# Starting the value projection on the first half of the features while the second half of the modulation row is still being summed

## What is computed

```python
cond = silu(c)                                   # one row of 2048
mod = cond @ mod_w[i] + mod_b[i]                 # 2048 x 6144, per layer i
shift, scale, gate = split(mod, 3)
h = rms_norm(x, norm_g[i]) * (1.0 + scale) + shift
# layer 0, pool_branch(h, w_in, w_grp, layer_scale, w_out):
v, gate_p = split(h @ w_in, 2)                   # 2048 -> 2 x 2048
pooled = window_mean(v) - v                      # four groups, windows 2, 4, 8, 16
mixed = per_group(pooled @ w_grp) * layer_scale  # four 512 x 512 matrices
x = x + gate * ((mixed * silu(gate_p)) @ w_out)
```

## Time and profile before

| | us |
|---|---|
| time, median of 3 runs | 2393.55 (2393.16 to 2394.4) |
| the profiled execution's own time | 2394.16 |
| its span | 2392.2 |
| PE busy | 2336.1 (98% of the span) |
| DVE busy | 1525.3 (64%) |
| ACT busy | 1116.2 (47%) |
| mean granted TensorE clock | 0.989 of full |

### The profile page before, as it was taken

The page is one execution under the profiler, slowest core; times in us unless marked ns, Lnnn a source line. Parts: engine busy times, 40 slices in busy tenths (PEclk is TensorE's granted clock), DMA queues, the critical chain, the costliest instruction groups (busy, mean ns, idle before and its releaser), DMA issues.

```text
span 2392.2 us, 29822 instructions
## 1 busy us (share of the span) xinstructions
PE 2336.1 (98%) x10938; PEld 1897.4 (79%) x10938; DVE 1525.3 (64%) x1837; ACT 1116.2 (47%) x1346; POOL 15.2 (1%) x21
## 2 busy tenths in 40 slices
PE   5999999999999999999999999998999999999997
PEld 1877777888788878888888888887888888888886
DVE  2988897666697566865664444655655565565555
ACT  2454445444444555545545444454544444444444
POOL 0000000000000000000000000000000000000000
PEclk8999998999999999999999999999999999999999
DMA  9999996555697545756455766555556656656653
GB/s 393 389 374 383 373 400 228 179 185 175 199 391 250 153 172 182 233 162 185 150 176 148 235 196 190 188 190 170 186 189 189 193 185 193 191 183 193 191 186 105
DMA packets 245077, 528.18 MB, mean 221 GB/s; under 512 B 20956, under 2 KB 21220, under 8 KB 241000
## 3 DMA queue, kind: packets, MB, share of 16 engines
q1 hardware_dynamic: 241376, 510.40, 64.3%
q0 software_dynamic: 1936, 13.67, 1.5%
q10 hardware_dynamic: 1656, 2.65, 0.3%
HBM read 520.35 MB, written 6.30 MB: 220 GB/s over the span
## 4 chain that ended last, share of the span: by engine, by line
PE 94%; DVE 2%; DMA 2%; ACT 1%; issue 1%; SPq 0%; DVEq 0%; ACTq 0%
PE ps L1890 29%; PE ps L1892 29%; PE ps L1891 29%; PE ps L1959 3%; DMA T<-in_mod_w 1%; PE ps L1989 1%; PE ps L2158 0%; DMA raw<-in_pool_w_in 0%; DVE w_lo L1040 0%; PE ps L2199 0%; PE ps L2060 0%; PE ps L2135 0%; ACT tmp L797 0%; PE ps L2201 0%; PE ps L2200 0%
## 5 line engine op out<-in xcount | busy, mean ns | idle before, releaser
L1040 DVE TENSOR_TENSOR w_lo<-raw,w_hi 128x1024 fp32r<-128x1024 f32 x784 | 945.4, 1218 | 480.7 <-ACT w_hi L514 464.3
L514 ACT CAST w_hi<-raw 128x1024 fp32r<-128x1024 f32 x784 | 814.8, 1046 | 832.1 <-PE ps L1892 798.8
L1890 PE MATMUL ps<-w_hi,xa_hi 128*128 128x512 f32 x2176 | 858.2, 394 | 6.1 <-DVE xa_lo L1074 2.7
L1892 PE MATMUL ps<-w_hi,xa_lo 128*128 128x512 f32 x2176 | 849.5, 390 | 0.0
L1891 PE MATMUL ps<-w_lo,xa_hi 128*128 128x512 f32 x2176 | 848.8, 390 | 0.0
L1890 PEld LDWEIGHTS ps<-w_hi,xa_hi 128*128 128x128 f32 x2176 | 409.6, 188 | 100.0 <-issue 11.2
L1892 PEld LDWEIGHTS ps<-w_hi,xa_lo 128*128 128x128 f32 x2176 | 409.3, 188 | 86.1
L1891 PEld LDWEIGHTS ps<-w_lo,xa_hi 128*128 128x128 f32 x2176 | 409.8, 188 | 82.7
L1890 PE MATMUL ps<-w_hi,xb_hi 128*128 128x512 f32 x928 | 365.6, 394 | 1.5 <-issue 1.1
L1892 PE MATMUL ps<-w_hi,xb_lo 128*128 128x512 f32 x928 | 361.8, 390 | 0.0
L1891 PE MATMUL ps<-w_lo,xb_hi 128*128 128x512 f32 x928 | 361.6, 390 | 0.0
(11 more groups left out here) (257 smaller groups left out, 963.8 us busy)
## 6 DMA issues: line engine op xcount, KB each, us to landing
raw<-in_w_in SPq DMA_DIRECT2D x176, 512.0 KB, 4.3
T<-in_mod_w SPq DMA_DIRECT2D x160, 512.0 KB, 7.6
...
raw<-in_w_up SPq DMA_DIRECT2D x128, 512.0 KB, 4.3
raw<-in_w_down SPq DMA_DIRECT2D x128, 512.0 KB, 4.4
...
```

What stands on the lines that cost most here:

```text
L514: nc.scalar.copy(w_hi[:, o % SPL, :, 0:cols], raw[:, o % RAW, :, 0:cols]).then_inc(hi_ready, 1)
L1040: tt(w_lo[:, o % SPL, :, part], raw[:, o % RAW, :, part], w_hi[:, o % SPL, :, part].bitcast(F32), ALU.subtract).then_inc(lo_ready, 1)
L1890: mm(dst, x_hi, h, start=first and k == 0, stop=False)
L1892: ins = mm(dst, x_lo, h, start=False, stop=last and k == KPC - 1)
```

## The change

It does five things.

1. The scale row is summed in 32 pieces of 512 KB: 16 for its first half (features 0 to 1023), then 16 for its second half, each in PE matmuls of 256 columns, in a ring of 8 slots. The value phase begins when the first half is there. Its first 16 chunks are reordered: features 0 to 1023 of column blocks 0 and 1 (places 0 to 3 and 4 to 7), then features 1024 to 2047 of both. The 16 pieces of the second half stand on PE behind places 0, 1, 2, 3 and 5, and the copy, columns and scale of the second half behind places 5 to 8.
2. The rotary tables are computed on DVE at the chunks 3 to 5, and their sines on ACT at chunk 8, no longer ahead of the scale row.
3. The rides of DVE begin at chunk 8 (before: 4) and those of the first row end at chunk 36 (before: 31). Of PE's rides 6 stand in `group` (before: 8).
4. The shift comes later: its totals stand behind chunk 37 (before: 33), its columns behind chunk 38 (before: 34), and `shift0` runs at the end of `group` and in the first block of `pool_gate`.
5. `awake(n)` puts n matmuls of 128 columns, whose result is not used, on PE: in the start, around the first transposes of `norm1`, and ahead of and behind the first transposes of the last norm, `norm3`.

```diff
--- before
+++ after
@@ -68,10 +68,11 @@
 def _rides():
     first = {name: PHASES[name][0] * CPB for name in ("pool_v", "group", "pool_gate")}
     v, gate = first["pool_v"], first["pool_gate"]
-    at = [v + c for c in range(4, 32) for _ in range(2 if c in (11, 17, 23, 28) else 1)]
+    at = [v + c for c in range(8, 32) for _ in range(2 if c in (13, 19, 25) else 1)]
+    at += [first["group"] + c for c in range(5)]
     at += [gate + i * 9 // 8 for i in range(32)]
     at += [gate + 36 + i * 27 // 32 for i in range(32)]
-    return at, [first["group"] + i for i in range(8)] + [gate + 1 + i * 60 // 24 for i in range(24)]
+    return at, [first["group"] + i for i in range(6)] + [gate + i * 62 // 26 for i in range(26)]
 
 
...
@@ -368,10 +369,15 @@
 
             mws = [mod_w[i].rearrange("(p k) (u n) -> p u k n", k=KC, n=D) for i in range(2)]
             sp.dma_start(csil[:], c[0].rearrange("(p k) -> p k", k=KC)).then_inc(c_landed, 16)
-            for k in range(KC):
-                if k >= 4:
-                    sp.wait_ge(mod_taken, k - 3)
-                sp.dma_start(mod_raw[:, k % 4, :], mws[0][:, 1, k, :]).then_inc(mod_landed[k % 4], 16)
+            def scale_piece(p):
+
+                if p >= 8:
+                    sp.wait_ge(mod_taken, p - 7)
+                c0 = p // KC * (D // 2)
+                sp.dma_start(mod_raw[:, p % 8, :], mws[0][:, 1, p % KC, c0:c0 + D // 2]).then_inc(mod_landed[p % 8], 16)
+
+            for p in range(KC):
+                scale_piece(p)
...
@@ -405,9 +411,15 @@
                 for b in range(n):
                     for j in range(CPB):
                         g = (B0 + b) * CPB + j
-                        load(SOURCES[name], b, j, B0 + b, first=g < RAW)
+                        if g < 2 * CPB:
+                            load(lambda b, j: SOURCES["pool_v"](g // 4 % 2, g // CPB * 4 + g % 4), b, j, B0 + b, first=g < RAW)
+                        else:
+                            load(SOURCES[name], b, j, B0 + b)
+                        if 2 <= g < 7:
+                            for p in range(KC + (0, 4, 7, 10, 13)[g - 2], KC + (4, 7, 10, 13, 16)[g - 2]):
+                                scale_piece(p)
                         for q in range(len(RIDE_CHUNK)):
-                            if g == (RAW - 1, RAW - 1, RAW + 2, RAW + 4)[q] if q < 4 else g == RIDE_CHUNK[q - 4] + RAW:
+                            if g == (RAW - 1, RAW - 1, RAW, RAW + 4)[q] if q < 4 else g == RIDE_CHUNK[q - 4] + RAW:
                                 ride_first(q)
                         for q in range(len(PE_CHUNK)):
                             if g == PE_ISSUE[q]:
...
+            blk(0, {2: norm0_start, 8: rotary_sines, 9: lambda: norm0(2)})
+            blk(1, {3: lambda: norm0(3), 7: lambda: pool_v(0), 9: lambda: pool_job(0)})
+            pool_v(1)
+            for b in range(2, 4):
+                blk(b, {6: lambda: pool_job(b - 1)})
+                pool_v(b)
 
             B0, A0, _ = PHASES["group"]
 
             def mixed(g):
-                act.wait_ge(mod_taken, KC + (2 if g < 2 else 4))
+                act.wait_ge(mod_taken, 2 * KC + (2 if g < 2 else 4))
                 evac(T1[:, :, g * NBLK:g * NBLK + NBLK], A0 + g, B0 * CPB + 2 * g + 2)
 
             def shift0(g):
                 act.wait_ge(shifted, g + 1)
-                nc.scalar.copy(XA[0][:, 4 * g:4 * g + 4, :], (tmp[:], stage_f)[g % 2]).then_inc(xh_ready, 1)
+                nc.scalar.copy(FIRST[0][:, 4 * g:4 * g + 4, :], (tmp[:], stage_f)[g % 2]).then_inc(xh_ready, 1)
 
             for o in range(AHEAD, CPB + AHEAD):
                 hi(B0, o)
...
@@ -1258,16 +1276,16 @@
                 step(ts(MODB[i], MODB[i], 1.0, None, ALU.add))
             dve.wait_ge(csil_ready, 1)
 
-            def scale_rows(i, bank, taken, of=mod_taken):
+            def scale_rows(bank, taken, of, at=0, n=NBLK):
 
                 dve.wait_ge(of, taken)
-                nc.vector.tensor_copy(mod_rows, ps[:, bank, :]).then_inc(rows_ready, 1)
-
-            def scale(i, sums, src, g):
+                nc.vector.tensor_copy(mod_rows[:, at:at + n], ps[:, bank, 0:n]).then_inc(rows_ready, 1)
+
+            def scale(i, sums, src, g, part=slice(0, KC)):
 
                 dve.wait_ge(mod_sum, sums)
-                step(tt(scl[:, i, :], src, MODB[i], ALU.add))
-                step(tt(scl[:, i, :], scl[:, i, :], g, ALU.mult))
+                step(tt(scl[:, i, part], src[:, part], MODB[i][:, part], ALU.add))
+                step(tt(scl[:, i, part], scl[:, i, part], g[:, part], ALU.mult))
                 dve.sem_inc(scl_ready, 1)
...
@@ -1286,21 +1304,29 @@
             def norm0_low(g):
                 low_job(SPLITS["norm0"] + g, XA, g, job_bank(g), scl[:, 0, :], 1 if g == 0 else 0)
 
-            scale_rows(0, 3, KC)
+            def scale_second():
+                scale(0, 2, ps[:, 7, 0:KC], G0, slice(8, KC))
+                norm0_low(2)
+
+            def turns_cos():
+                rotary_turns(cos, 0.25)
+
+            scale_rows(3, KC, mod_taken, 0, S)
             lo(0, 0)
-            scale(0, 1, ps[:, 2, 0:KC], G0)
+            scale(0, 1, ps[:, 2, 0:KC], G0, slice(0, 8))
             norm0_low(0)
             lo(0, 1)
             norm0_low(1)
             lo(0, 2)
-            B0 = PHASES["pool_v"][0]
-            for b in range(4):
-                first_blk(B0 + b, {6: lambda: low_job(SPLITS["pool_v"] + b - 1, XB, b - 1, 4)} if b else
-                          {3: lambda: norm0_low(2), 5: lambda: norm0_low(3)})
+            first_blk(0, {3: rotary_angles, 4: turns_cos, 5: rotary_last, 8: lambda: scale_rows(6, 2 * KC, mod_taken, S, S),
+                          9: scale_second})
+            first_blk(1, {3: lambda: norm0_low(3), 10: lambda: low_job(SPLITS["pool_v"], XB, 0, 4)})
+            for b in range(2, 4):
+                first_blk(b, {6: lambda: low_job(SPLITS["pool_v"] + b - 1, XB, b - 1, 4)})
 
 
             def first_shift():
-                dve.wait_ge(mod_sum, 2)
+                dve.wait_ge(mod_sum, 3)
                 step(nc.vector.tensor_copy(vec3[:, 0:KC], ps[:, 6, 0:KC]))
...
@@ -1332,8 +1357,7 @@
                     shift0(g + 2)
 
             first_blk(PHASES["group"][0], {
-                4: shift_rows, 5: shift0_start, 6: lambda: shift0_next(0),
-                7: lambda: shift0_next(1), 8: lambda: shift0_next(2), 9: lambda: shift0_next(3)})
...
@@ -2032,19 +2057,30 @@
                              start=True, stop=True)
                 ins.then_inc(mod_sum, 1)
 
-            hooks = feed("norm0", 0, xn)
+            def awake(n):
+
+                for _ in range(n):
+                    mm(ps[:, 1, 0:P], ident, ident, start=True, stop=True)
+
+            def scale_sum(p, bank):
+                mod_piece(p % KC, mod_raw[:, p % 8, :], bank, 0, S, mod_landed[p % 8], 16 * (p // 8 + 1), p % KC == 0)
+
             pe.wait_ge(csil_ready, 1)
+            pe.wait_ge(con_landed, 16)
             for k in range(KC):
-                mod_piece(k, mod_raw[:, k % 4, :], 3, 0, NBLK, mod_landed[k % 4], 16 * (k // 4 + 1), k == 0)
-                if k == 7:
+                scale_sum(k, 3)
+                if k == 12:
                     pe.wait_ge(vec_landed, 16 * 13)
-                    pe.wait_ge(con_landed, 16)
                     nc.tensor.transpose(ps[:, 4, 0:104], stage[0:104, 0, 0:P], ident[0:104, 0:104])
                     nc.tensor.transpose(ps[:, 5, 0:96], stage[0:96, 1, 0:P], ident[0:96, 0:96]).then_inc(vec_tp, 1)
-                if k == 11:
+                if k == 14:
                     pe.wait_ge(vec_done, 1)
-                    hooks.pop(-1)()
-            mod_columns(1, 2, 0, False)
+                    norm_job("norm0", 0, xn, 0)
+                    norm_job("norm0", 0, xn, 1)
+                if k > 9:
+                    awake(1 if k < KC - 1 else 4)
+            mod_columns(1, 2, 0, True, (0, 1))
+            awake(5)
...
+                if g == 0:
+                    pe.wait_ge(tp_evac, JOBS["norm0"] + 2)
+                for p in {0: range(16, 20), 1: range(20, 23), 2: range(23, 26), 3: range(26, 29), 5: range(29, 32)}.get(g, ()):
+                    scale_sum(p, 6)
+                if g == 1:
+                    norm_job("norm0", 0, xn, 2)
+                if g == 6:
+                    mod_columns(2, 7, 0, True, (2, 3))
+                if g == 7:
+                    pe.wait_ge(scl_ready, 2)
+                    norm_job("norm0", 0, xn, 3)
+                if g == 13:
+                    pool(0)
+            for b in range(2, 4):
+                blk(b, b, XA, True, {3: lambda: pool(b - 1)})
             B0, A0, _ = PHASES["group"]
             for j in range(CPB):
                 if j % 2 == 0:
...
@@ -2071,11 +2129,10 @@
                 chunk(B0, j, XB, KPC * j, A0 + j // 2, j % 2 == 0, j % 2 == 1)
                 if j == 0:
                     pool(3)
-                if j == 1:
-                    pe.wait_ge(tp_evac, JOBS["pool_v"] + 3)
```

(21 more changed lines are left out.)

70 lines of the change are left out of this document (38 added, 32 removed).

## The result

The changed kernel took 2411.06 us (median of 4 runs, 2409.02 to 2413.22) against 2393.86 of before: a ratio of 1.0071 with a 95% interval of 1.0058 to 1.0083. It is slower, on the side that was forecast, and by 17.2 us where 5.3 were forecast. The profiled execution is the slowest of the four (2413.22); its span of 2411.4 is 19.2 longer than before's. Three single executions fell into a slow state (2627 us of the kernel before, 3591 in experiment 11, 4781 in experiment 13); they move the medians given here by at most 0.2 us, and the ratios leave them out.

The account below looks back on a forecast made before the run. PE, busy throughout the first block, was taken as the bound there, so only chunk 0's delay by the 16 MB scale row could be won. Terms 1.0 + 4.3 + 1.5 - 1.5 + 0 = +5.3 on 2393.55 gave 2399, range 2391.5 to 2407.

Parts of the forecast that it names:

- the fourth rival: DVE stays behind after the stall or half clock lasts twice as long: 6 to 13 us more, 2405 to 2412, chance 0.10.
- own range: The range from adding all terms' low ends (-0.9) and high ends (13.6), given as 2396 to 2406.7.
- the two waits that it named: PE idle about 8 us ahead of chunk 7, ended by DVE's copy, and 4 us ahead of chunk 40.
- Chunk 0 comes earlier: At the start, chunk 0 needs only the scale row's first half, so begins at 37.2, 20.4 us earlier than 57.60.
- Rides of DVE and PE keep their number ... 12% idle covers their tighter spacing: From 57.60 to 385.50 DVE's 12% idle (40 us) covers the rides' tighter spacing; put at nothing.
- A wait that the change adds: Value phase: DVE's first ride waits for the bias until S + 8.5, chunk 7 at about S + 10.6; phase total +1.0.
- the rival's price of 6.2 us kept: First rival: DVE's ride does not wait for the bias ahead of chunk 7; 6.2 us more kept, 2392.7, chance 0.15.
- The shift: Ahead of chunk 40, DVE's chain of 7.0 us is covered only by chunk 39's 2.7: +4.3.
- The clock: Behind the idle stretch ahead of chunk 40, PE runs at half clock for 3 to 7 us: +1.5.
- no clock time of its own: The idle stretch ahead of chunk 7 costs nothing through the clock, since DVE's chain sets chunks 8 and 10.
- The norms: Matmuls of no use return half-clock time at `norm1`, -1.5; at `norm3` DVE is the limit, 0.

Follow-up runs that it names:

- experiment 11: The changed kernel without points 3 and 4 (row 0's rides in chunks 8 to 31), with DVE's first two rides behind the scale's second half; 2397.61 us.
- experiment 13: The kernel before with only the matmuls of no use around the first transposes of the second layer's norm; 2394.60 us against 2393.55.
- experiment 9: The kernel before with only PE's rides as the change has them, six in the group phase and 26 behind it; 2395.90 us against 2394.78.
- Experiment 12: The changed kernel without the matmuls of no use at the start, those at the two norms kept; 2411.18 us.
- Experiments 1: The changed kernel with the load of DVE's fourth ride behind the load of chunk 16 in SP's queue, no longer chunk 12; 2405.67 us.
- 4: The changed kernel with PE's fifth and sixth ride loads one chunk earlier in SP's queue, behind the load of chunk 43; 2408.10 us.
- experiment 10: The changed kernel without points 3 and 4, row 0's rides in chunks 8 to 31 with eight doubled; 2404.98 us.
- edit 2: DVE's first two rides moved behind the second half of the scale and the low part of group 2; alone on the changed kernel 2404.65 us.
- Experiment 2: The changed kernel with DVE's first two rides behind the second half of the scale and the low part of group 2; 2404.65 us.
- experiment 5: The changed kernel with the shift two chunks earlier (totals behind chunk 35, columns behind chunk 36), rides as they are; 2402.21 us.
- 7: The kernel before with only points 3 and 4 of the change, the later rides and the later shift; 2402.02 us.
- 8: The kernel before with the later rides and PE's later pieces, the shift two chunks earlier than the change has it; 2396.95 us against 2394.78.
- 6: The changed kernel with DVE's first two rides and its fourth ride's load later, PE's fifth and sixth ride loads and the shift earlier; 2398.02 us.

## Why the prediction went wrong in size

The time lies outside the range (2391.5 to 2407). It is that of the fourth rival, "more is lost" (2405 to 2412, chance 0.10): rides late for longer than to chunk 14 are a part of what happened. The prediction's "own range" of 2396 to 2406.7 is a slip: its ends of -0.9 and +13.6 give 2392.7 to 2407.2. The sign and the two waits that it named were right; the start was mis-sized and the tighter rides and pieces were put at nothing. In the profiled execution:

| term | forecast | measured |
|---|---|---|
| chunk 0 | 37.2 | 41.6 |
| last piece summed, S | 65.7 | 68.5 |
| PE's wait ahead of chunk 7 | 7.9 | 7.8 |
| chunk 7 behind S | 10.6 | 11.7 |
| chunk 14 against before | +1.0 | +5.5 |
| chunk 14 to 32 | 0 | +0.9 |
| wait ahead of chunk 37, half clock behind it | 0 | +3.8 and +1.7 |
| wait ahead of chunk 40 | +4.3 | +4.4 |
| half clock behind it | +1.5 | +1.7 |
| PE's moved pieces, net (experiment 9) | 0 | +1.7 |
| second layer's norm | -1.5 | -1.5 |
| last norm | 0 | +0.0 |

From "chunk 14 against before" down these add up to 18.2 of the 19.2 us; the other 1.0 is in no term. Against the 5.3 of the forecast the start misses 4.5, and what was put at nothing 8.1.

**"Chunk 0 comes earlier": mis-sized by 4.4 us.** The step took the last half piece as landed at 30.2 because 8 MB had landed then before. It landed at 33.7: the queues moved 335 and 340 GB/s from 16 to 20 and 20 to 24 us (405 and 403 before), and three chunk loads issued at 23.0 to 24.3 were under way beside it. By 33.7 they had moved 12.3 MB, before by 30.2 only 11.4, so other loads' bytes took part of the time. What slowed them between 16 and 24 us stays open. PE then took 7.9 us to chunk 0 where 7.0 were forecast. Of the 4.4 us 2.8 are left at S, since from chunk 0 to S it took 27.0 us, not 28.5: PE waited 0.96 us ahead of the first piece of the second half, where the sum had 3.9, a term that no row gives. Chunk 7 is 3.9 later than forecast and chunk 14 4.3. Experiment 12 shows no effect of the matmuls of no use beyond the scatter of the start.

**"Rides of DVE and PE keep their number ... 12% idle covers their tighter spacing": the step that failed.** An average of idle time was taken as cover, and no queue was followed behind the load that waits. The prediction priced DVE's first ride, but not a ride's load that waits on SP (the fourth's, for the transposes of group 3), nor what SP has behind it. In place of nothing the runs showed +0.9 from chunk 14 to 32, then PE's wait of 3.8 us for a piece ahead of chunk 37, with 1.7 of half clock. Experiments 1 and 4 show SP's queue as its cause: 5.4 and 3.0 us by moving loads in that queue alone (both take away the wait ahead of chunk 37, so they don't add up). The same sentence hid the pieces (1.7 us in the trace of experiment 9, not to be told in its time) and, in experiment 10, the denser rides without edit 2 (7.7 us over 18 chunks, but 1.4 in experiment 11).

**"A wait that the change adds": right.** The bias, DVE's ride, the copy, PE's columns, in that order and with that length. Experiment 2 took it away and chunk 7 was 8.9 us sooner. The median fell by 6.4 us, near the rival's price of 6.2 us kept, but by luck: only 4.9 us of it were there at chunk 14.

**"The shift": right to 0.1 us**, shown by experiment 5 and twice on the kernel before (7 and 8). **"The clock": right.** Where PE had waited 3.8 and 4.4 us the matmuls behind ran at half clock for 3.4 us each time; 1.7 us, where 1.5 were forecast for one place. Ahead of chunk 7 "no clock time of its own" is nearly right for chunk 8 (it began 0.7 behind DVE's low part), but the clock was at half there too (0.59 from 77.5 to 86.5): chunk 7 took 5.0 us in place of 2.7, and the transposes that SP's held load waits for stand behind it. An estimate from this: 2.3 us of the empty queues are the clock's.

**The norms.** At the last norm PE's clock was full, and DVE was the limit as forecast:

```profile
1676.00:1679.00 3.00, 2.71 (x23) 2.52 (x24) 2.17 (x10) 0.83 (x3) 0.55 (x1) 1.00 0.56 184
```

```profile
1678.78 5.39 DVE L1824 SCALAR_TENSOR_TENSOR T<-T,rs 128x512 f32<-128x512 f32 x8
1684.08 1.66 DVE L1095 SCALAR_TENSOR_TENSOR xb_lo<-ps,vec,xb_hi 128x256 fp32r<-128x256 f32 x4
```

The term of the second layer's norm has the right size in the trace; that the added matmuls are its cause isn't shown (last section).

**Did the early start pay at all?** Not in any version here: with the bias out of the way it is even at chunk 14 (experiment 2), and behind by 3 in others (6 and 11). The reading of experiment 2, that the pieces use up the queues while DVE has nothing to split and DVE then lacks the time, fits all of these; it is argued from the windows, and no run here took DVE's load away. No version with the early start was as fast as the kernel before.
